# Slot 1's expert weights by a list, issued from Pool's queue; slot 0's second half behind the first gather

## The chip, the cores and the metric

One core of one Trainium2 chip. The metric is the device time of the kernel in microseconds (us). Its five engines are named as in the profile: PE (TensorE, matmuls), DVE (VectorE), ACT (ScalarE), POOL (GpSimd) and SP (SyncE, here only an issuer of DMAs). A "q" behind an engine (ACTq) is its instruction queue.

## The reference, cut to what matters

The whole kernel computes two blocks of two layers each (attention, convolution, gating mixers). The change touches only the mixture-of-experts part, which runs twice (l = 0 and l = 1), each time on 1024 tokens of width 1024 with 32 experts in four groups, two experts of one group for each token:

```python
def moe_ffn(h, w_rg, b_rg, w_re, b_re, w_gate, w_up, w_down):
    ...
    expert = g_idx[:, None] * EXPERTS_PER_GROUP + top_i.astype(jnp.int32)
    ...
    def expert_block(args):
        xblk, e = args
        hid = jax.nn.silu(xblk @ w_gate[e]) * (xblk @ w_up[e])
        return hid @ w_down[e]

    yb = lax.map(expert_block, (xb, block_e)).reshape(n_rows, d)
    return jnp.zeros_like(h).at[row_tok].add(yb * row_w[:, None])
```

w_gate and w_up are 1024x512 for each expert, w_down 512x1024, all float32. Which expert a token takes depends on the data, so the kernel computes its tables on the chip.

## The kernel before

**Tiling.** The 2048 assignments are cut into blocks of 64 rows that share one expert, experts with most blocks first. Counting the assignments of the reference on its inputs gives, for l = 0, 50 blocks (17 experts with one block, 12 with two, 3 with three), and for l = 1, 48 blocks (20, 8 and 4 experts). The blocks are worked off in rounds of two: in round j slot 0 takes block j from the heavy end, slot 1 takes block n + j, where n is the number of rounds (25 and 24). Slot 0 so works through experts of two and three blocks, slot 1 through experts of mostly one.

**Weights.** Each slot has one buffer for one expert: first half of gate and up (a, 2048 KB), second half (b, 2048 KB), down (d, 2048 KB). `load_gu` (L2298) and `load_dn` (L2303) issue them. There is no second buffer: a part can be loaded only when the last matmuls that read it are done. PE counts that in `free_a`, `free_b` and `free_d` (they start at 2 and grow by one for each slot in each round).

**SP** (`blocks_sp`) loads slot 0 from a list: one entry for each new expert, with its expert number (AT_E) and its place (AT_POS). That is 11 loads of a, b, d for l = 0 and 10 for l = 1. With rounds counted from 0, slot 0 takes a new expert in rounds 0, 3, 6, 9, 11, 13, 15, 17, 19, 21, 23 (l = 0) and 0, 3, 6, 9, 12, 14, 16, 18, 20, 22 (l = 1).

**ACT** (`round_act`) loads slot 1 anew in every round, 49 times in all, whether the expert changes or not: a right after slot 1's a matmuls, b right after its b matmuls, d after its down matmuls. It also applies Silu, copies half of the turned rows, and stores the results (`store_y`, four DMAs of 128 KB a round, L2379).

**Pool** (`blocks_pool`) gathers the 128 token rows of a round (512 KB, indirect DMA, L2315, its index copied at L2312) into the one buffer xb, as soon as PE has turned the rows before (semaphore `xt`).

**PE** (`blocks_pe`) does in each round: gate and up of slot 0 (a, then b), of slot 1 (a, then b), all at L2345; the turning of `hid` (L2352) and of the next round's rows (`turn_x`, L2329); down of slot 0, down of slot 1 (L2362). Each part waits for its weights with a count that comes from a table (slot 0, AT_RANK) or from the round number (slot 1).

**Tables.** `route_dve` and `route_pe` build them before the rounds from the counts: `fresh` marks a block with a new expert on slot 0, a matmul with `before` ranks them, `one_l` turns them into lists, and PE puts the lists into one row (L2092 to L2094) that DVE copies to `moe_tab`. `in_blk` and `at_off` (L2100) give the token rows of each block, `moe_i` the place at which `sum_pool` later picks each result up.

## Time and profile before

| | us |
|---|---|
| median of 3 runs | 4387.5 |
| lowest, highest | 4382.78, 4392.72 |
| the profiled execution | 4384.98 |
| its span, first to last instruction | 4383.2 |

| engine | busy us | share of the span |
|---|---|---|
| PE | 3946.5 | 90% |
| DVE | 1444.3 | 33% |
| ACT | 898.6 | 21% |
| POOL | 125.6 | 3% |

The rounds of l = 0 run from 2526.2 to 3143.6 of the span, those of l = 1 from 3718.6 to 4310.0. All DMAs together move 693.44 MB. PE's busy share says little by itself: it is an average over stages, and a matmul at half clock counts as busy for twice as long. What the change can do is read from the two stretches of rounds: how long a round takes in which nothing is waited for, and which rounds are longer.

### The profile page before, as it was taken

The numbers are of one execution on the slowest core, as the hardware profiler recorded it, in microseconds if no ns is written. First come the engines' busy times: TensorE is split into PE (matmuls) and PEld (weight loads), VectorE is DVE, ScalarE is ACT, GpSimd is POOL, SyncE is SP. The second block draws the span as 40 slices with busy tenths as digits, with TensorE's granted clock in tenths as the row PEclk, the third lists the DMA queues.
The fourth block names the chain that finished last, engine by engine and source line by source line (L and its number), as shares of the span: only waits on it lengthen the run. The fifth ranks groups of instructions, "written<-read, shape, count | busy, mean of one in ns | idle before, by whom it ended". The sixth has DMA issues, their size and how long they took to land.

```text
span 4383.2 us, 48965 instructions
## 1 busy us (share of the span) xinstructions
PE 3946.5 (90%) x19350; PEld 1970.3 (45%) x19351; DVE 1444.3 (33%) x2688; ACT 898.6 (21%) x1885; POOL 125.6 (3%) x203
## 2 busy tenths in 40 slices
PE   4997888899999889999988799999799997999986
PEld 2555665454444555444664333333344443333333
DVE  2485666313302663252463411111231114111115
ACT  3003454202001332121152211111120002111111
POOL 0000000000000000000000000000100000000001
PEclk8998999999999999999999899999899998999997
DMA  6310222110101000110240299999711103999995
GB/s 244 136 39 36 94 94 112 44 42 33 62 20 39 1 1 10 48 46 30 97 156 20 84 399 378 426 426 424 312 36 39 39 21 130 385 391 392 420 423 200
DMA packets 81279, 693.44 MB, mean 158 GB/s; under 512 B 9696, under 2 KB 11560, under 8 KB 45408
## 3 DMA queue, kind: packets, MB, share of 16 engines
q10 hardware_dynamic: 39824, 342.78, 19.0%
q1 hardware_dynamic: 23168, 280.66, 16.0%
q0 software_dynamic: 18128, 67.77, 4.2%
q8 instruction: 114, 1.87, 0.2%
q14 instruction: 45, 0.37, 0.0%
HBM read 636.11 MB, written 55.05 MB: 158 GB/s over the span
## 4 chain that ended last, share of the span: by engine, by line
PE 44%; DMA 11%; DVE 4%; issue 1%; ACT 1%; POOL 0%; ACTq 0%; DVEq 0%; POOLq 0%
PE banks L259 22%; PE banks L2345 12%; DMA arena<-in_w_gu 10%; PE banks L2362 5%; PE banks L1476 1%; DMA arena<-y_tok,arena 1%; DVE arena L1591 1%; PE banks L2329 1%; PE banks L2067 1%; PE banks L2352 1%; DMA arena<-h_tok,arena 1%; PE banks L466 1%; PE banks L1545 0%; PE banks L1525 0%; DVE banks L1590 0%
## 5 line engine op out<-in xcount | busy, mean ns | idle before, releaser
L259 PE MATMUL banks<-arena 128*128 128x512 f32 (+2 forms) x4544 | 1752.2, 547 | 50.4 <-ACTq L138 28.7
L259 PEld LDWEIGHTS banks<-arena 128*128 128x128 f32 x4544 | 841.6, 191 | 950.4 <-issue 887.5
L2345 PE MATMUL banks<-arena 128*64 128x512 f32 x3136 | 718.4, 615 | 70.8 <-DMA arena<-in_w_gu 68.5
L2345 PEld LDWEIGHTS banks<-arena 128*64 128x64 f32 x3136 | 231.4, 142 | 548.2 <-issue 456.8
L2362 PE MATMUL banks<-arena 128*64 128x512 f32 x1568 | 349.2, 598 | 3.2 <-issue 3.2
L1545 PE MATMUL banks<-arena 128*64 128x128 f32 x1952 | 162.1, 285 | 54.5 <-ACT arena L1558 39.3
L2362 PEld LDWEIGHTS banks<-arena 128*64 128x64 f32 x1568 | 109.0, 137 | 208.5 <-issue 208.5
L939 DVE SCALAR_TENSOR_TENSOR arena<-arena 128x1024 f32<-128x1024 f32 x240 | 195.9, 878 | 0.2 <-DVEq L138 0.2
L2435 DVE COPY arena<-banks 128x256 f32<-128x256 f32 x98 | 41.1, 420 | 414.4 <-PE banks L2352 414.4
L1476 PE MATMUL banks<-arena 64*128 64x256 f32 (+2 forms) x768 | 130.1, 469 | 37.8 <-ACT arena L1647 32.8
L301 DVE SCALAR_TENSOR_TENSOR arena<-banks,arena 128x512 f32<-128x512 f32 (+1 forms) x72 | 51.9, 721 | 333.7 <-PE banks L259 333.7
L1525 PE MATMUL banks<-arena 128*128 128x128 f32 x976 | 150.5, 285 | 1.9 <-ACT arena L1647 1.9
L1545 PEld LDWEIGHTS banks<-arena 128*64 128x64 f32 x1952 | 103.2, 136 | 106.0 <-ACT arena L1558 78.3
L2431 DVE TENSOR_TENSOR arena<-arena,banks 128x256 f32<-128x256 f32 x98 | 40.8, 416 | 325.4 <-ACT arena L2385 325.4
L272 ACT ACTIVATE arena<-banks 128x512 f32<-128x512 f32 (+1 forms) x43 | 24.1, 559 | 577.5 <-PE banks L259 577.5
L2439 DVE COPY arena<-banks 128x512 f32<-128x512 f32 x49 | 33.9, 692 | 324.1 <-PE banks L2362 324.1
L1273 PE MATMUL banks<-arena 128*128 128x128 f32 x800 | 109.4, 285 | 34.5 <-DVE arena L1364 34.5
L1647 ACT ACTIVATE arena<-banks,arena 128x1024 f32<-128x1024 f32 (+3 forms) x144 | 135.2, 939 | 23.0 <-DVE arena L1593 22.1
L1591 DVE TENSOR_REDUCE arena<-banks 128x1 f32<-128x1024 f32 (+3 forms) x144 | 135.4, 940 | 13.2 <-PE banks L1476 9.5
L1525 PEld LDWEIGHTS banks<-arena 128*128 128x128 f32 x976 | 104.8, 142 | 55.4 <-issue 50.1
L280 ACT ACTIVATE arena<-banks 128x512 f32<-128x512 f32 (+1 forms) x68 | 38.0, 559 | 424.6 <-PE banks L259 424.5
L1558 ACT ACTIVATE arena<-banks 128x512 f32<-128x512 f32 (+1 forms) x160 | 90.6, 566 | 163.5 <-PE banks L1525 162.2
(341 smaller groups left out, 3075.3 us busy)
## 6 DMA issues: line engine op xcount, KB each, us to landing
arena<-in_w_gu ACTq DMA_DIRECT2D x98, 2048.0 KB, 14.0
arena<-in_w_dn ACTq DMA_DIRECT2D x49, 2048.0 KB, 13.2
arena<-in_w_gu SPq DMA_DIRECT2D x42, 2048.0 KB, 12.3
arena<-in_w_ada SPq DMA_DIRECT2D x24, 2048.0 KB, 7.3
arena<-in_w_dn SPq DMA_DIRECT2D x21, 2048.0 KB, 14.9
y_tok<-arena ACTq DMA_DIRECT2D x196, 128.0 KB, 12.7
y_tok<-arena POOLq DMA_DIRECT2D x1, 16384.0 KB, 45.2
arena<-in_ab_w_ada SPq DMA_DIRECT2D x6, 2048.0 KB, 9.4
```

The costliest lines, as they stand in the source:

```text
L259: last = pe.matmul(self.bank_of(g, n), lhsT, rhs, start=k == 0, stop=k == KT - 1)
L301: d.scalar_tensor_tensor(out=grp.dst, in0=src, scalar=grp.more["gate"], in1=grp.dst, op0=ALU.mult, op1=ALU.add).then_inc(proj_ev["D"], 1)
L939: d.scalar_tensor_tensor(out=out, in0=src, scalar=wt, in1=out, op0=ALU.mult, op1=ALU.add).then_inc(conv_n, 1)
L1273: last = pe.matmul(bank(7)[:, 0:V.shape[1]], self.PT[0:K, g % self.n_pt, 128 * j:128 * j + 128], V, start=g == mine[0] and j == 0, stop=g ...
L1476: ins = pe.matmul(banks[:, c0:c0 + k.shape[1]], q, k, start=True, stop=True)
L1525: ins = pe.transpose(self.tbank(g)[:, 128 * j:128 * j + 128], self.P[u % 2][s_][:, c0:c0 + P], ident)
L1545: ins = pe.matmul(bank(7)[64 * s_:64 * s_ + 64, 0:128], V, self.PT[g % len(self.PT)][:, 128 * j:128 * j + 128], start=g == mine[0] and j < ...
L1558: last = eng.tensor_copy(o, s_) if which == "D" else eng.activation(o, s_, ACT.Copy)
L1591: link(d.tensor_reduce(st[:, s_:s_ + 1], sc[:, 0:un["n"]], X_AXIS, ALU.max))
L1647: a.activation(self.P[i % 2][s_][:, 0:un["n"]], self.scores(s_)[:, 0:un["n"]], ACT.Exp, bias=st[:, 2 + s_:3 + s_], scale=un["scale"][s_][0 ...
L2345: last = pe.matmul(bank(2 + s_)[64 * h:64 * h + 64, :], xbT[:, k, 64 * s_:64 * s_ + 64], w_gu[s_][:, k, h], start=k == 0, stop=k == KT - 1 ...
L2362: last = pe.matmul(bank(6 + s_)[64 * h:64 * h + 64, :], hidT[:, s_, ch % 2, 64 * (ch // 2):64 * (ch // 2) + 64], w_dn[s_][:, ch, 512 * h:5 ...
```

## The change

- The blocks of slot 1 run backwards: in round r it takes block 2n - 1 - r instead of n + r, so from the light end. Equal experts of slot 1 so still stand side by side, but the experts with two blocks come last.
- `fresh`, the ranks and the lists are made for both slots. Slot 1's list has, besides the expert and the first round of each entry, the round behind its last one (AT_END). Slot 1 is loaded only for a new expert.
- ACT loads no weights any more, and its round has one form. Pool issues slot 1's weights: after the gathers of the rounds that an entry covers, a and b when `free_a` and `free_b` allow it, then d when `free_d` does.
- The gather of round j + 2 stands in iteration j, behind `xt` j + 2; one more gather is issued at the end of each stage (27 and 26 instead of 26 and 25).
- On SP, part b of slot 0 waits for the first gather (`xg` 16); in later iterations that wait is always met.
- PE waits for slot 1's weights by a rank from the table, as for slot 0.
- The tables need some more small steps on DVE (`n_last`, `before_of`, a second `one_l`, `held`, the ranks, and five for the new place of each result) and slightly other matmuls.

```diff
@@ route_pe
+                both_l = one_l.rearrange("p a b -> p (a b)")
+                for at_, col in ((AT_E, exp_id), (AT_POS, place[:, 0:1])):
+                    pe.matmul(bank(7)[0:1, at_:at_ + 2 * LOADS], col, both_l, start=True, stop=True)
+                pe.matmul(bank(7)[0:1, AT_END:AT_END + LOADS], place[:, 0:1], one_l[:, 1], start=True, stop=False)
+                pe.matmul(bank(7)[0:1, AT_END:AT_END + LOADS], place[:, 1:2], held, start=False, stop=True)
...
@@ route_dve
-                link(d.tensor_scalar(blk_of, side, rounds_n[0:NBLK], first_round, ALU.mult, ALU.add))
+                link(d.tensor_scalar(n_last, rounds_n, 2.0, -1.0, ALU.mult, ALU.add))
+                link(d.tensor_scalar(blk_of, side, n_last[0:NBLK], from_end, ALU.mult, ALU.add))
+                link(d.scalar_tensor_tensor(out=before_of, in0=side, scalar=2.0, in1=blk_of, op0=ALU.mult, op1=ALU.add))
...
-                link(d.tensor_scalar(one_l, c("iota", NBLK)[:, 0:LOADS], rank, fresh, ALU.is_equal, ALU.mult))
-                d.tensor_tensor(rank, rank, fresh, ALU.add).then_inc(m_oh, 1)
+                for s_ in range(2):
+                    link(d.tensor_scalar(one_l[:, s_], c("iota", NBLK)[:, 0:LOADS], rank2[:, s_:s_ + 1],
+                                         fresh2[:, s_:s_ + 1], ALU.is_equal, ALU.mult))
+                link(d.tensor_tensor(rank2, rank2, fresh2, ALU.add))
+                link(d.tensor_scalar(held, c("iota", NBLK)[:, 1:LOADS + 1], rank2[:, 1:2], valid, ALU.is_equal,
+                                     ALU.mult))
+                link(d.tensor_tensor(rank, rank2[:, 1:2], rank2[:, 0:1], ALU.subtract))
+                d.tensor_scalar(rank, rank, side, rank2[:, 0:1], ALU.mult, ALU.add).then_inc(m_oh, 1)
...
+                link(d.tensor_scalar(places[:, 1], iota_r, -1.0, n_last, ALU.mult, ALU.add))
...
@@ blocks_sp
                     for part, landed, free in ((0, self.wa[0], self.free_a), (1, self.wb[0], self.free_b)):
+                        if part == 1:
+                            sp.wait_ge(self.xg, 16)
                         sp.wait_ge(landed, 16 * j + 16)
                         sp.sem_inc(self.passed, 1)
-                        sp.wait_ge(free, pos + 1)
+                        sp.wait_ge(free, 2 * pos + 1)
...
@@ blocks_pool
-                with g.Fori(0, n) as j:
-                    g.wait_ge(self.xt, j + 1)
-                    self.gather(g, j + 1)
+                more = g.value_load(moe_tab[0:1, AT_ROUNDS + 1:AT_ROUNDS + 2], min_val=1, max_val=LOADS - 1)
+                e = g.value_load(moe_tab[0:1, AT_E + LOADS:AT_E + LOADS + 1], min_val=0, max_val=E - 1)
+                g.wait_ge(self.xt, 1)
+                self.gather(g, 1)
+                for part in range(2):
+                    self.load_gu(g, 1, e, part)
+                self.load_dn(g, 1, e)
+                with g.Fori(0, more) as i:
+                    first = g.value_load(moe_tab[0:1, bass.ds(AT_POS + LOADS + i, 1)], min_val=0, max_val=ROUNDS - 1)
+                    end = g.value_load(moe_tab[0:1, bass.ds(AT_END + i, 1)], min_val=1, max_val=ROUNDS)
+                    e = g.value_load(moe_tab[0:1, bass.ds(AT_E + LOADS + 1 + i, 1)], min_val=0, max_val=E - 1)
+                    with g.Fori(first, end) as j:
+                        g.wait_ge(self.xt, j + 2)
+                        self.gather(g, j + 2)
+                    for part, free in ((0, self.free_a), (1, self.free_b)):
+                        g.wait_ge(free, 2 * end + 2)
+                        g.sem_inc(self.passed, 1)
+                        self.load_gu(g, 1, e, part)
+                    g.wait_ge(self.free_d, 2 * end + 2)
+                    g.sem_inc(self.passed, 1)
+                    self.load_dn(g, 1, e)
...
@@ blocks_pe
-                    rank_ = pe.value_load(moe_tab[0:1, bass.ds(AT_RANK + 2 * j, 1)], min_val=1, max_val=LOADS)
-                    need = [16 * rank_ + 16, 16 * j + 16]
+                    ranks = [pe.value_load(moe_tab[0:1, bass.ds(AT_RANK + 2 * j + s_, 1)], min_val=1, max_val=LOADS)
+                             for s_ in range(2)]
+                    need = [16 * ranks[0] + 16, 16 * ranks[1]]
...
@@ round_act, blocks_act
-                if not last:
-                    a.wait_ge(self.free_a, 2 * j + 4)
-                    self.load_gu(a, 1, e, 0)
...
-                if not last:
-                    self.load_gu(a, 1, e, 1)
...
-                if not last:
-                    a.wait_ge(self.free_d, 2 * j + 4)
-                    self.load_dn(a, 1, e)
...
```

## Rows read from the trace of the kernel before

**Rows 1.** The page, part 4: the chain that ended last, by line.

```profile
PE banks L259 22%; PE banks L2345 12%; DMA arena<-in_w_gu 10%; PE banks L2362 5%; PE banks L1476 1%; DMA arena<-y_tok,arena 1%; DVE arena L1591 1%; PE banks L2329 1%; PE banks L2067 1%; PE banks L2352 1%; DMA arena<-h_tok,arena 1%; PE banks L466 1%; PE banks L1545 0%; PE banks L1525 0%; DVE banks L1590 0%
```

**Rows 2.** Waits of the whole kernel: who for whom: us in total, times, longest.

```profile
PE banks L2345 <- DMA arena<-in_w_gu: 68.5, 24, 4.3
```

**Rows 3.** Windows: rounds of each layer, rounds after the first, single stretches.

```profile
core 0: us, PE busy (x) PEld busy (x) DVE busy (x) ACT busy (x) POOL busy (x), PEclk, DMA share, GB/s
2526.20:3143.60 617.40, 579.40 (x2700) 205.79 (x2700) 71.49 (x149) 79.81 (x124) 28.48 (x49) 0.97 0.97 405
3718.60:4310.00 591.40, 557.66 (x2592) 197.07 (x2592) 68.61 (x143) 76.46 (x119) 27.43 (x47) 0.97 0.95 393
2550.20:2988.50 438.30, 414.64 (x1946) 146.97 (x1944) 51.97 (x108) 58.38 (x90) 20.73 (x36) 0.98 0.98 408
3743.70:4258.80 515.10, 485.60 (x2272) 172.13 (x2270) 60.64 (x126) 68.12 (x105) 24.13 (x42) 0.97 0.97 401
2839.00:2889.80 50.80, 46.96 (x220) 16.39 (x218) 5.78 (x12) 6.49 (x10) 2.31 (x4) 0.97 1.01 426
2608.68:2615.30 6.62, 6.62 (x17) 1.80 (x18) 0.00 (x0) 0.00 (x0) 0.00 (x0) 0.55 1.03 434
```

**Rows 4.** Timeline of a quiet round: start, length (us), engine, line, operation.

```profile
2550.20 13.90 PE L2345 MATMUL banks<-arena 128*64 128x512 f32 x64
2550.55 0.34 ACTq L2303 DMA_DIRECT2D arena<-in_w_dn  x1
2560.85 0.35 ACTq L2298 DMA_DIRECT2D arena<-in_w_gu  x1
2564.30 0.34 ACTq L2298 DMA_DIRECT2D arena<-in_w_gu  x1
2564.31 1.04 PE L2329 MATMUL banks<-arena 128*128 128x128 f32 x8
2565.68 7.09 PE L2362 MATMUL banks<-arena 128*64 128x512 f32 x32
2566.49 0.97 POOL L2315 DMA_INDIRECT arena<-h_tok,arena  x1 [0.79 <-POOL arena L2312]
2572.60 1.46 PE L2345 MATMUL banks<-arena 128*64 128x512 f32 x6
```

**Rows 5.** Timeline of the next round: SP's loads of slot 0.

```profile
2576.45 3.77 SPq L2298 DMA_DIRECT2D arena<-in_w_gu  x2
2591.99 0.33 SPq L2303 DMA_DIRECT2D arena<-in_w_dn  x1
```

**Rows 6.** Timeline of the round after that: the stall.

```profile
2608.68 6.62 PE L2345 MATMUL banks<-arena 128*64 128x512 f32 x16 [3.21 <-DMA arena<-in_w_gu]
```

**Rows 7.** DMA issues at 2634.4 and 2507.4 alone: last column, us to landing.

```profile
arena<-in_w_gu ACTq DMA_DIRECT2D x1, 2048.0 KB, 7.2
...
arena<-in_w_gu SPq DMA_DIRECT2D x1, 2048.0 KB, 8.1
```

**Rows 8.** DMA queues from 2576 to 2606: packets, MB, share.

```profile
q1 hardware_dynamic: 431, 6.29, 49.4%
q0 software_dynamic: 144, 0.52, 4.3%
```

**Rows 9.** The page, part 6: issues of gate and up halves, median us to landing.

```profile
arena<-in_w_gu ACTq DMA_DIRECT2D x98, 2048.0 KB, 14.0
arena<-in_w_gu SPq DMA_DIRECT2D x42, 2048.0 KB, 12.3
```

**Rows 10.** Timeline ahead of the first round of layer 1.

```profile
2499.77 0.14 DVE L2240 COPY arena<-banks 64x1 f32<-64x1 f32 x1
2505.92 3.63 PE L2100 MATMUL banks<-arena 128*64 128x33 f32 x64 [3.01 <-DVE arena L2258]
2511.01 1.05 POOL L2315 DMA_INDIRECT arena<-h_tok,arena  x1 [0.87 <-POOL arena L2312]
2522.89 1.97 PE L2329 MATMUL banks<-arena 128*128 128x128 f32 x8 [13.35 <-DMA arena<-h_tok,arena]
```

More of the change, by code:

```diff
@@ L2217, in route_dve @@
                 link(d.tensor_copy(ends, bank(7)[:, 0:65]))
-                first_round, side = (c("place", NBLK)[:, i:i + 1] for i in range(2))
+                first_round, side, from_end = (c("place", NBLK)[:, i:i + 1] for i in range(3))
                 upto = ends[0:NBLK, 32:64]
@@ L2320, in blocks_pool @@
                 n = self.rounds(g)
-                with g.Fori(0, n) as j:
-                    g.wait_ge(self.xt, j + 1)
-                    self.gather(g, j + 1)
+                more = g.value_load(moe_tab[0:1, AT_ROUNDS + 1:AT_ROUNDS + 2], min_val=1, max_val=LOADS - 1)
[19 more added lines that the diff above has]
+                    self.load_dn(g, 1, e)
+                first = g.value_load(moe_tab[0:1, bass.ds(AT_POS + LOADS + more, 1)], min_val=0, max_val=ROUNDS - 1)
+                with g.Fori(first, n) as j:
+                    g.wait_ge(self.xt, j + 2)
+                    self.gather(g, j + 2)
+                g.wait_ge(self.xg, 16 * n + 32)
+                g.sem_inc(self.passed, 1)
             def turn_x(self, pe, j):
```

100 lines of the change are left out of this document (46 added, 54 removed).

## The prediction

> **What bounds the kernel now.** I read the chain that ended last first: outside the dense projections (L259) it runs through the expert matmuls L2345 (12%) and L2362 (5%) and through the DMA of `in_w_gu` (10%) [rows 1]. So both PE and the weight loads end stretches of the rounds. The waits then say how much PE really idled for them: 68.5 us in 24 waits, none over 4.3 us [rows 2]. The windows give the size of the whole matter. The rounds take 617.4 and 591.4 us [rows 3]. A quiet round is 22.40 us, from 2550.20 to 2572.60 [rows 4], and 49 of them are 1097.6 us. So 1208.8 - 1097.6 = 111.2 us are lost in the rounds, and no change of the loads alone can win more than these.
>
> Where they are lost: in the windows without the first round, 18 rounds of l = 0 take 438.3 us, 35.1 over the quiet time, with 7 reloads of slot 0; 21 rounds of l = 1 take 515.1, 44.7 over, with 8 reloads [rows 3]. That is 79.8 us, **5.3 us for each of 15 reloads**. The other 31.4 us lie in the two first rounds and around the last four reloads. A stall looks so: the second half of slot 1 comes 3.21 us late [rows 6], and behind it 6.62 us run at a granted clock of 0.55, near the lower of the two levels (1.2 and 2.4 GHz) [rows 3]; before, PE had been idle for those 3.21 us. 68.5 us of waits and some 43 us of slow matmuls make the 111.
>
> Two rounds with one reload take 50.8 us at 426 GB/s and a DMA share of 1.01 [rows 3]: there the transfers themselves are the bound. Over the first 18 rounds after the opening the rate is 408: where the reloads are three rounds apart, there is room, and stalls come from order, not from amount.
>
> **The clock of a round.** From the quiet round [rows 4], counted from its start: PE's four quarters of L2345 end at 3.5, 6.9, 10.4 and 13.9 (13.90 in four equal parts); the turning of rows ends at 15.2 (2565.35); down begins at 15.5, its second half at 19.0. Slot 1's loads are issued at 10.7 (a), 14.1 (b) and 0.4 of the next round (d). The gather is issued from 16.3 to 17.3. SP issues a at 3.9 and, within that row of 3.77 us, b at about 7.3, and d at 19.4 [rows 5]. Weights are due: slot 1's a at 6.9, b at 10.4, d at 19.0; slot 0's a at 0. A load alone lands 7.2 to 8.1 us after its issue [rows 7]; 2048 KB at 426 GB/s are 4.9, so 2.3 to 3.2 are fixed. I take 1.6 ahead of the first byte and 1.3 behind the last, near the upper end, because the row of SP is the load that nothing shared with. When two queues hold loads, each gets about half (the medians are 14.0 and 12.3 us against 7.2 alone [rows 9]).
>
> **Part 1: slot 1's a and b leave later.** Today ACT issues them right after the quarter that frees the buffer. In the new order Pool must first wait for the turning of the rows and issue the gather, which ends at 17.3. The two loads follow: Pool's price for issuing a plain 2048 KB load is not in these rows; its bounds are ACT's 0.34 and the gather's 0.97 us [rows 4]. I take 0.9, nearest to the row of the same engine. So a leaves at 18.2 instead of 10.7 and b at 19.0 instead of 14.1: **7.5 and 5 us later**, in a round in which both are due 11 and 14 us after that. They also stand on one queue behind the gather, and d of this round behind them.
> - A round with nothing from SP: gather 18.9 to 20.1, a to 25.0, b with the y stores (0.52 MB, 1.2 us) to 31.2, landing 26.3 and 32.5; due 29.3 and 32.8. No stall, but only 0.3 us to spare for b.
> - The round ahead of a reload (SP issues at 3.9 and 7.3): b has 2.7 us left to move when SP's a enters at 5.5. At half rate, with stores, it lands near 13; due 10.4, stall 2.7. d follows at half rate, 11.8 to 21.7, lands at 23.0; due 19.0 + 2.7, stall 1.3 to 1.7. Neither is long enough for a lower clock, if the stall of 3.21 us is the measure. Together **4.4**, and this round has no loss today.
> - The reload round: SP's b and d are still moving while the gather and slot 1's a want to. The gather has small packets (0.52 MB in 144, against 6.29 MB in 431 on SP's queue [rows 8]) and, packet by packet in turn, is pushed to about 28; a moves at half rate beside SP's d and lands at 37.8 from the start of the round before, due at 26.8 + 6.9 = 33.7. Stall 4.1, then slow matmuls: 43 us over 19 reloads are 2 us each. Together **6.0**.
>
> So 10.4 us for a reload instead of 5.3, and over 15 reloads 156 - 79.8 = **+76 us**. The same by amount: behind the reload round all loads are done some 5 us before Pool issues the next gather, and in a stretch where the DMAs are the bound those 5 us are lost.
>
> **Part 2: fewer loads.** Backwards, slot 1's 25 rounds of l = 0 hold 17 single experts and four of two rounds: 21 loads. For l = 1 it is 20 and two: 22. 43 instead of 49, each 6.29 MB, 14.8 us at 426 GB/s. But the six that go lie in rounds 18, 20, 22, 24 and 21, 23, behind the stretch where the DMAs are the bound. In the last four reloads (19, 21, 23 and 22) both slots want weights in the same round: a of slot 1, leaving at 18.2 beside SP's d, lands 1.8 late, b 3.1 late, with 2 for the clock 6.8, so 27 us for four. Today they and the two first rounds lose 31.4. I take **0**; the ends are -27 (all gone) and +14.
>
> **Part 3: the start.** Today the gather is issued at 2511.0 beside three loads of slot 0 and PE starts at 2522.9, 13.35 us idle [rows 10]. With only a ahead of it the rows land near 2516.5, 6 us sooner. But b of slot 0 leaves then, and slot 1's a waits for the turning and for gather 1, whose small packets stand beside SP's b and d: it moves from about 2527 and lands near 2535.5, where today the second quarter ends at 2534. The 6 us become a stall of about 7 plus slow matmuls. **+3.5 for each l, +7**; ends -4 and +10.
>
> **Part 4: the tables.** Ahead of the release of the rounds stand 6 more chained steps on DVE: the row at 2499.77 is 0.14 long and the next is chained at 0.18 [rows 10], some 0.22 with its wait. 1.3 us for each l, **+2.6**. The five steps for the place of the results lie beside PE's 3.63 us at 2505.92 [rows 10]; without that cover they would cost 1.1 each time. ACT's loop gets lighter, but ACT is not waited for. The extra gather at the end lies beside the last round. SP's new wait holds only SP's own b and d, priced in part 3.
>
> **Sum.** 76 + 0 + 7 + 2.6 = +86 on the profiled execution's 4385.0: 4471. The median of the runs shown is 2.5 above it: **4473 us**, own range 4440 to 4505 (the fixed part of a load 2.3 instead of 2.9, or Pool's issue 0.5 us slower, moves it by some 10 each; the ends of parts 2 and 3 by some 25).
>
> **Rivals.**
> - *The later issue is hidden by what is queued.* At a DMA share of 1.01 it should not matter when a load joins the queue. Then only the six loads and the last four reloads count: -27 and +2.6, 4363. For: the two-round stretch. Against: SP's two halves are all that is queued at 18, and rounds with nothing from SP are quiet until 17. The Trainium skill ("DMA: Bandwidth & Descriptors", section "Issuing engines are not separate DMA queues") says that the issuing engine saves only issue time, since all share 16 DMA engines; by it the move to Pool is neutral. Chance 0.13. That even the other 84 us go, 4280: 0.02.
> - *Half of it.* Backlog covers the lateness where reloads are two rounds apart, and only the seven reloads three rounds apart lose 5: +35 with parts 3 and 4 and less of part 2, 4420. Chance 0.08, with 4388, no difference, inside its lower edge.
> - *Slower still: Pool's packets are smaller than SP's.* Pool's gathers average 3.6 KB, SP's loads 14.6 [rows 8]. If Pool's weight loads are cut to half of SP's packets, slot 1 gets a third beside SP instead of half. b is then 6.4 late in the round ahead of a reload (8.3 with the clock), and a 3.2 late after it (5.1): 13.4 instead of 10.4, +45, 4518. It decides once the packets differ by two. No plain load of such rows by Pool is in these rows. Chance 0.13.
> - *Forecast* 0.64.
>
> **How the numbers follow.** The likeliest is 4473. Leaving out the 0.15 on the fast side and the tails gives 4410 to 4530. A measurement of this kernel can tell 0.2% (8.8 us) from no change: faster 0.15, same 0.02, slower 0.83.
>
> **What the profile after would show.** Queue q0 with some 339 MB, q10 with 34 (342.78 less 49 times 6.29), 37.7 MB less in all; Pool's loads at about 18 and 19 of a round; new waits of L2345 and L2362 in the round ahead of each reload, near 27 us, and reload rounds near 28.5; rounds 18, 20, 22 at 22.4. Wrong, if the round ahead of a reload stays at 22.4 (then the backlog covers it), or if Pool's a leaves before 15.

## The result, and the profile after

| | before | changed kernel |
|---|---|---|
| median us | 4385.14 (4 runs, 4374.65 to 4392.72) | 4459.68 (4 runs, 4458.66 to 4460.59) |
| the profiled execution | 4384.98 | 4459.17 |
| its span | 4383.2 | 4457.3 |

The ratio is 1.0172, 95% interval 1.015 to 1.0194: the changed kernel is 74.5 us slower. The forecast was 86 slower, 4473. The time is 13 below it and inside the range.

From the page of the changed kernel: PE's busy time, and two of the DMA queues (packets, MB, share). L2388 is now the gate and up matmul, L2405 down, L2371 the turning of rows, L2333 the gather, L2319 and L2324 the weight loads.

```profile
PE 3965.0 (89%) x19354; PEld 1981.0 (44%) x19355; DVE 1448.0 (32%) x2710; ACT 900.9 (20%) x1886; POOL 200.6 (5%) x337
...
q0 software_dynamic: 36992, 339.36, 19.0%
...
q10 hardware_dynamic: 18656, 34.49, 2.2%
```

Queue q0 carries 339.36 MB and q10 34.49, as the prediction had them. All DMAs together move 656.74 MB instead of 693.44, so 36.7 MB less. The prediction said 37.7, because it left out the two extra gathers of 0.52 MB. **Less is moved and it takes longer**: PE is only 18.5 us busier over the whole span, the rest of the loss is idle time. PE's waits for gate and up weights went from 68.5 us [rows 2] to

```profile
PE banks L2388 <- DMA arena<-in_w_gu: 106.9, 24, 8.7
```

in as many waits, the longest twice as long. Where they lie, the windows say (stretch, us, then each engine's busy time, granted clock, DMA share, GB/s): the rounds of l = 0 and of l = 1, their rounds after the first up to the last stretch (two lines), the last stretches (two lines), and in the end a quiet round, the round ahead of a reload and the reload round.

```profile
2520.10:3177.00 656.90, 592.58 (x2700) 212.15 (x2700) 71.47 (x149) 80.69 (x125) 64.70 (x114) 0.94 0.85 349
3748.10:4380.50 632.40, 567.54 (x2592) 202.82 (x2592) 68.66 (x143) 77.51 (x120) 65.06 (x115) 0.95 0.86 355
2553.10:3021.50 468.40, 423.24 (x1946) 152.32 (x1944) 51.96 (x108) 58.39 (x90) 48.82 (x87) 0.95 0.90 372
3782.50:4328.80 546.30, 494.32 (x2270) 177.67 (x2268) 60.61 (x126) 68.12 (x105) 57.23 (x102) 0.96 0.90 370
3021.50:3177.00 155.50, 142.24 (x650) 50.73 (x646) 17.32 (x36) 19.46 (x30) 10.94 (x19) 0.93 0.70 278
4328.80:4380.50 51.70, 47.65 (x218) 16.48 (x214) 5.76 (x12) 6.49 (x10) 2.88 (x5) 0.93 0.49 187
2553.10:2575.50 22.40, 22.40 (x110) 8.11 (x108) 2.89 (x6) 3.24 (x5) 2.80 (x5) 1.00 0.82 332
2575.50:2599.50 24.00, 22.55 (x110) 8.21 (x108) 2.88 (x6) 3.24 (x5) 2.80 (x5) 1.00 1.00 424
2599.50:2628.80 29.30, 24.32 (x110) 8.69 (x108) 2.89 (x6) 3.24 (x5) 2.80 (x5) 0.94 0.89 363
```

Against [rows 3]: 468.4 instead of 438.3 us and 546.3 instead of 515.1, so +61.3 us for the same 15 reloads. DMA share and rate fell from 0.98 and 408 GB/s to 0.90 and 372. The last stretches are 0.4 and 0.5 longer than before (155.1 and 51.2). In all rounds, span less PE busy is 129.2 us of idle time, before 71.7: +57.5. PE's busy time is 1160.1 against 1137.1: +23.0, the same matmuls at a lower clock.

The timeline of these three rounds (start, length, engine, line, operation, idle time ahead and who ended it):

```profile
2570.40 1.09 POOL L2319 DMA_DIRECT2D arena<-in_w_gu  x2
2591.79 0.99 POOL L2333 DMA_INDIRECT arena<-h_tok,arena  x1 [0.79 <-POOL arena L2330]
2592.79 1.09 POOL L2319 DMA_DIRECT2D arena<-in_w_gu  x2
2594.89 0.33 SPq L2324 DMA_DIRECT2D arena<-in_w_dn  x1
2596.09 3.65 PE L2405 MATMUL banks<-arena 128*64 128x512 f32 x16 [1.45 <-issue]
2599.54 7.07 PE L2388 MATMUL banks<-arena 128*64 128x512 f32 x32
2611.48 8.82 PE L2388 MATMUL banks<-arena 128*64 128x512 f32 x32 [4.87 <-DMA arena<-in_w_gu]
```

Pool issues a and b right behind the gather (2570.40), 17.3 and 17.8 us after the round's start. In the next round the same group leaves at 2592.79, when SP's b (issued at 2582.8) still moves and SP's d is about to join (2594.89). a should be there for the third quarter at 2606.6. It is there at 2611.48, 4.87 us late; the 32 matmuls behind it take 8.82 us instead of 7. In the round ahead, the second half of down starts 1.45 us late. The view names no releaser, but slot 1's d lands at 2596.00, right ahead of it. And because PE is late, the next gather is issued only at 2622.69, when everything queued has been moved: the channels nearly stand still from 2621.6 to 2624.6 (19 GB/s).

```profile
2621.60:2624.60 3.00, 3.00 (x16) 1.12 (x18) 1.01 (x2) 0.58 (x1) 2.08 (x4) 1.00 0.21 19
```

How long the gather takes (last column: us to landing; the quiet round's gather and the reload's):

```profile
arena<-h_tok,arena POOLq DMA_INDIRECT x1, 4.4
...
arena<-h_tok,arena POOLq DMA_INDIRECT x1, 11.3
```

The 512 KB of rows land in 4.4 us alone and in 11.3 beside SP's loads, as the prediction had expected from its small packets (said to be pushed to 28 of the round before, measured 27.6).

### The profile page after: what moved, and what is told of

Read it like the earlier page. It is cut to its first block, busy times and chain, and to the rows that moved or that the text cites. A ratio compares the mean times of both kernels' runs of the same rounds, so it can differ in the third digit from the quotient of the medians.

```text
span 4457.3 us, 49754 instructions
## 1 busy us (share of the span) xinstructions
PE 3965.0 (89%) x19354; PEld 1981.0 (44%) x19355; DVE 1448.0 (32%) x2710; ACT 900.9 (20%) x1886; POOL 200.6 (5%) x337
## 2 busy tenths in 40 slices
DMA packets 78976, 656.74 MB, mean 147 GB/s; under 512 B 9441, under 2 KB 11305, under 8 KB 45409
## 3 DMA queue, kind: packets, MB, share of 16 engines
q0 software_dynamic: 36992, 339.36, 19.0%
q1 hardware_dynamic: 23168, 280.66, 15.8%
q10 hardware_dynamic: 18656, 34.49, 2.2%
## 4 chain that ended last, share of the span: by engine, by line
PE 44%; DMA 11%; DVE 4%; issue 2%; ACT 1%; POOLq 1%; POOL 0%; DVEq 0%; ACTq 0%
PE banks L259 22%; PE banks L2388 12%; DMA arena<-in_w_gu 10%; PE banks L2405 4%; PE banks L2371 1%; PE banks L1476 1%; DMA arena<-y_tok,arena 1%; DVE arena L1591 1%; PE banks L2395 1%; PE banks L2071 1%; PE banks L466 1%; DMA arena<-h_tok,arena 0%; PE banks L1545 0%; PE banks L1525 0%; POOLq L138 0%
## 5 line engine op out<-in xcount | busy, mean ns | idle before, releaser
L2388 PE MATMUL banks<-arena 128*64 128x512 f32 x3136 | 740.3, 630 | 109.0 <-DMA arena<-in_w_gu 106.9
L2388 PEld LDWEIGHTS banks<-arena 128*64 128x64 f32 x3136 | 242.4, 146 | 597.4 <-issue 453.8
L2405 PE MATMUL banks<-arena 128*64 128x512 f32 x1568 | 350.8, 596 | 22.1 <-issue 22.0
L2405 PEld LDWEIGHTS banks<-arena 128*64 128x64 f32 x1568 | 110.1, 137 | 227.8 <-issue 227.8
L2434 ACT ACTIVATE arena<-banks 128x256 f32<-128x256 f32 x98 | 37.6, 383 | 639.7 <-PE banks L2388 639.7
L1476 PE MATMUL banks<-arena 64*128 64x256 f32 (+2 forms) x768 | 130.2, 470 | 37.7 <-ACT arena L1647 32.8
L1545 PEld LDWEIGHTS banks<-arena 128*64 128x64 f32 x1952 | 103.0, 136 | 106.7 <-ACT arena L1558 78.4
L272 ACT ACTIVATE arena<-banks 128x512 f32<-128x512 f32 (+1 forms) x43 | 24.1, 559 | 579.0 <-PE banks L259 579.0
L1558 ACT ACTIVATE arena<-banks 128x512 f32<-128x512 f32 (+1 forms) x160 | 90.6, 566 | 164.4 <-PE banks L1525 162.3
## 6 DMA issues: line engine op xcount, KB each, us to landing
arena<-in_w_gu POOLq DMA_DIRECT2D x86, 2048.0 KB, 14.8
y_tok<-arena ACTq DMA_DIRECT2D x196, 128.0 KB, 10.4
```

Of the source, the lines that this page charges most:

```text
L1476: ins = pe.matmul(banks[:, c0:c0 + k.shape[1]], q, k, start=True, stop=True)
L1545: ins = pe.matmul(bank(7)[64 * s_:64 * s_ + 64, 0:128], V, self.PT[g % len(self.PT)][:, 128 * j:128 * j + 128], start=g == mine[0] and j < ...
L1558: last = eng.tensor_copy(o, s_) if which == "D" else eng.activation(o, s_, ACT.Copy)
L2388: last = pe.matmul(bank(2 + s_)[64 * h:64 * h + 64, :], xbT[:, k, 64 * s_:64 * s_ + 64], w_gu[s_][:, k, h], start=k == 0, stop=k == KT - 1 ...
L2405: last = pe.matmul(bank(6 + s_)[64 * h:64 * h + 64, :], hidT[:, s_, ch % 2, 64 * (ch // 2):64 * (ch // 2) + 64], w_dn[s_][:, ch, 512 * h:5 ...
```

## The experiments

All times are medians, with the ratio to the runs of before on the same chip. "Reload" is a reload round less 22.4 us, mean over the 15 reloads of the two long windows; "ahead" is the same for the round before it (before: 5.3 and 0.0; changed kernel: 7.6 and 1.8); "last four" is the sum over the last four reloads (before 26.8, changed kernel 27.5).

### Lateness alone, on ACT's queue

The kernel before, with slot 1's a and b issued behind ACT's copy of the turned rows.

```diff
-                if not last:
-                    a.wait_ge(self.free_a, 2 * j + 4)
-                    self.load_gu(a, 1, e, 0)
                 a.wait_ge(self.free_b, 2 * j + 4)
                 ...
-                if not last:
-                    self.load_gu(a, 1, e, 1)
                 self.copy_x(a, "A", j + 1)
+                if not last:
+                    a.wait_ge(self.free_a, 2 * j + 4)
+                    for part in range(2):
+                        self.load_gu(a, 1, e, part)
```

> The kernel before with one move: ACT issues slot 1's a and b (still in every round, still on its own queue) behind its copy of the turned rows instead of right behind each quarter. They leave at about 16 of a round instead of 10.7 and 14.1. Theory of lateness: the round ahead of a reload and the reload round together lose 8 to 9 us over 44.8 instead of 5.3; over 19 reloads 35 to 65 us slower than before. Rival, Pool's queue (software descriptors, one queue for gather, a, b and d) is the cause of the loss: nothing is moved to Pool here, so within 9 us of before. Rival, the backward order and the list are the cause: within 9 us of before too.

4415.08 us, ratio 1.0067 (1.005 to 1.0084): 31.5 slower. Reload 7.1, ahead 0.0, last four 32.8. In the round ahead of the first reload, a and b leave 15.3 and 15.8 us after its start; in the changed kernel it is 17.3 and 17.8, so this run tests most of the lateness and not all of it. The windows: the rounds of both layers.

```profile
2525.90:3163.70 637.80, 587.00 (x2700) 206.24 (x2700) 71.46 (x149) 79.83 (x124) 28.45 (x49) 0.96 0.95 392
3736.00:4341.10 605.10, 562.11 (x2592) 198.02 (x2592) 68.59 (x143) 76.44 (x119) 27.42 (x47) 0.96 0.93 384
```

Idle time of the rounds is 93.8 us, 22.1 more than before, and PE is busy 12.0 longer. So a load that joins the queue later is not hidden by what stands in it: the backlog rival is wrong. But this much lateness on ACT's queue gives less than half of the loss, and it never reaches the round ahead of a reload.

### Pool's queue alone, and Pool late

Weights for every round as before (no list), a and b on Pool when their part comes free, gather and d behind them. ACT issues no weights any more, and slot 1's first three loads leave behind the second gather:

```diff
@@ blocks_pool
+                with g.Fori(0, before) as j:
+                    e = self.expert(g, j + 1)
+                    for part, free in ((0, self.free_a), (1, self.free_b)):
+                        g.wait_ge(free, 2 * j + 4)
+                        g.sem_inc(self.passed, 1)
+                        self.load_gu(g, 1, e, part)
+                    g.wait_ge(self.xt, j + 2)
+                    self.gather(g, j + 2)
+                    g.wait_ge(self.free_d, 2 * j + 4)
+                    g.sem_inc(self.passed, 1)
+                    self.load_dn(g, 1, e)
```

> The kernel before, slot 1 still loaded in every round and in forward order, but all its loads issued by Pool, a and b as early as ACT did (behind their quarters, ahead of the gather), d behind the gather; the first three leave behind gather 1. Theory of lateness: the rounds lose about what they lose before, 95 to 125 us over the quiet time in all, so 4375 to 4400. Rival, Pool's queue is the cause: 60 us or more above before, near 4445 to 4460, with a stall of a in each reload round.

4366.93 us, ratio 0.9956 (0.9941 to 0.997): 16.6 **faster** than before. Reload 3.7, ahead 0.0, last four 25.8. The second kernel only moves the turning's wait and the gather ahead of a and b, where the change has them:

```diff
                     e = self.expert(g, j + 1)
+                    g.wait_ge(self.xt, j + 2)
+                    self.gather(g, j + 2)
                     for part, free in ((0, self.free_a), (1, self.free_b)):
                     ...
                         self.load_gu(g, 1, e, part)
-                    g.wait_ge(self.xt, j + 2)
-                    self.gather(g, j + 2)
```

> As the run above, but the gather ahead of a and b, as in the changed kernel; still 49 loads in forward order, no list. Theory of lateness: rounds 1 to 18 (l = 0) and 1 to 21 (l = 1) lose what they lose in the changed kernel, some 9.4 us for each of 15 reloads, and the last four reloads 9.4 each as well: 4460 to 4480, 0 to 15 above the changed kernel. Rival, the list with its backward order is the cause: near before, 4375 to 4400.

4474.79 us, ratio 1.0203 (1.0186 to 1.022). Reload 7.4, ahead 2.0, last four 47.5 (their rounds ahead included). The windows of the rounds of both layers: Pool early with its first reload round, then that reload round of before, then Pool late.

```profile
2527.80:3143.70 615.90, 575.51 (x2700) 203.21 (x2700) 71.45 (x149) 80.74 (x125) 69.59 (x124) 0.98 0.97 407
3719.00:4291.90 572.90, 543.82 (x2592) 192.91 (x2592) 68.58 (x143) 77.56 (x120) 66.83 (x119) 1.00 0.97 406
2599.80:2625.80 26.00, 22.61 (x110) 7.95 (x108) 2.88 (x7) 3.25 (x5) 2.79 (x5) 1.00 1.01 430
```
```profile
2595.00:2623.90 28.90, 25.69 (x112) 8.77 (x110) 2.89 (x6) 3.24 (x5) 1.15 (x2) 0.88 1.01 426
```
```profile
2531.40:3200.60 669.20, 596.62 (x2700) 212.48 (x2700) 71.46 (x149) 80.77 (x125) 70.02 (x124) 0.95 0.90 374
3776.50:4404.10 627.60, 566.70 (x2592) 202.68 (x2592) 68.57 (x143) 77.51 (x120) 67.25 (x119) 0.95 0.89 371
```

**The order on Pool costs 108 us** (4366.9 to 4474.8) with every load still made and on one queue. That is the change's loss, and more than it. Pool early against before shows something else. Idle time in the rounds is 69.5 us against 71.7, nearly the same, and so is the rate in the reload round (430 and 426 GB/s). What is shorter is PE's busy time, 1119.3 against 1137.1. In the first reload round the stall is 3.4 us (26.00 less 22.61 busy) and the clock stays at 1.00, where before a stall of 3.2 was followed by matmuls at 0.55 [rows 3, 6].

One pair of rounds doesn't tell the whole. Over the 15 reload rounds of the two long windows, the granted clock lies below 1.00 in 11 before and in 3 with Pool early (in the changed kernel in all 15). And the waits have another form. Before, the wait for slot 1's second half takes 2.5 to 3.9 us (in 3 rounds with a shorter one for its first half ahead of it). With Pool early PE waits twice in 8 of the 15, for slot 0's second half and for slot 1's, mostly under 2 us each, and in 5 of the other 7 the one wait takes 1.8 to 2.2 us. A round of l = 1:

```profile
4100.50 7.09 PE L2359 MATMUL banks<-arena 128*64 128x512 f32 x32 [1.84 <-DMA arena<-in_w_gu]
4109.48 3.65 PE L2359 MATMUL banks<-arena 128*64 128x512 f32 x16 [1.90 <-DMA arena<-in_w_gu]
```

So the waits of a reload are cut into shorter pieces (3.0 us in all on average, before 3.5), and the clock falls less often. That the shorter pieces are the cause is not shown: in the kernel before, one wait of 3.9 us (round 16 of l = 1) left the clock at 1.00, and in the kernel with all of slot 1 on Pool's queue, shown further down, one of 2.0 us (round 9 of l = 1) was followed by 0.94 over the round.

### The gather behind the late weights

As the kernel before it (Pool late), but only the wait for the turning stays ahead; the gather follows a and b.

```diff
                     g.wait_ge(self.xt, j + 2)
-                    self.gather(g, j + 2)
                     for part, free in ((0, self.free_a), (1, self.free_b)):
                     ...
                         self.load_gu(g, 1, e, part)
+                    self.gather(g, j + 2)
```

> As the run with Pool late and no list (4474.8): a and b still wait for the turned rows, but the gather is issued behind them instead of ahead. Splits what lateness on ACT's queue left open (31 us there, 91 with Pool late). If the gather's small packets ahead of a on one queue are the other part: a reload costs 6 to 7.5 us instead of 9.4, total 4415 to 4445. Rival, Pool's queue with d behind a and b is that part (or the late issue alone, to be read as 9.4 on any queue): above 4460.

4453.1 us, ratio 1.0162 (1.0134 to 1.019). Both expectations fell: the time lies between. Reload 7.1, ahead 1.3. Of the loss in the rounds against Pool early (90.9 us over quiet rounds there, 176.9 here, 198.9 with the gather ahead), 86 come from leaving late and 22 from the gather ahead of the weights on the same queue. Leaving late cost only 34 on ACT's queue (from 111 over quiet rounds before to 145). One difference lies in the round ahead of a reload: there the second half of down starts 1.3 us late on average in this kernel and in time in the one on ACT's queue. Here d stands behind a, b and the gather on one queue, there the gather has a queue to itself. No run separates that from the 0.7 us by which a and b also leave later here (16.0 instead of 15.3).

### The wait at the start

The changed kernel without SP's wait for the first rows.

```diff
-                        if part == 1:
-                            sp.wait_ge(self.xg, 16)
```

> The changed kernel without SP's wait of slot 0's second half for the first gather. Only the start of the rounds can differ. By the working of the start: the first gather again shares with three loads, PE starts some 6 us later (near 2526), slot 1's first a leaves later too, the stall in front of it is shorter: total 0 to 6 us above the changed kernel. Rival, the wait costs what the first round has lost (33 us against 24): 5 to 15 us below the changed kernel.

4460.32 us, ratio 1.0176 (1.0159 to 1.0193). From SP's first issue to round 1 it takes 44.3 and 45.9 us, with the wait 45.3 and 46.1, before 42.8 and 43.1. The wait moves TensorE's start 6 us earlier and gives it all back in the first round:

```profile
2507.83 9.85 SPq L2319 DMA_DIRECT2D arena<-in_w_gu  x2
2517.07 1.97 PE L2371 MATMUL banks<-arena 128*128 128x128 f32 x8 [7.00 <-DMA arena<-h_tok,arena]
2521.09 1.15 POOL L2319 DMA_DIRECT2D arena<-in_w_gu  x2
```

This is the changed kernel's start. SP's line of 9.85 us is its a and, behind the wait, its b. The rows are there after 7.00 us of idling instead of 13.35 [rows 10], but slot 1's first weights leave at 2521.09, behind the turning and the second gather.

### The last gather

The changed kernel without the extra gather at the end of each stage.

```diff
-                with g.Fori(first, n) as j:
+                with g.Fori(first, n - 1) as j:
                     g.wait_ge(self.xt, j + 2)
                     self.gather(g, j + 2)
-                g.wait_ge(self.xg, 16 * n + 32)
+                g.wait_ge(self.xg, 16 * n + 16)
```

> The changed kernel without the one gather that it adds at the end of each stage (its rows are used by nothing). Pool's drain of 7.6 us behind that gather ended 2 us after ACT's. If it holds the stage back: 2 to 3 us less for each l, 4453 to 4456. Rival, ACT's stores set the stage's end anyway: within 1 us of the changed kernel.

4454.25 us, ratio 1.0162 (1.0134 to 1.019), 5.4 below the changed kernel's median. The timeline at the end of l = 1: in the changed kernel the last matmuls and the first gather of the results, and then that gather in this kernel and in the kernel before.

```profile
4377.77 2.75 PE L2405 MATMUL banks<-arena 128*64 128x512 f32 x12
4387.34 0.95 POOL L2470 DMA_INDIRECT arena<-y_tok,arena  x1 [12.12 <-POOLq L138]
```
```profile
4383.95 0.97 POOL L2470 DMA_INDIRECT arena<-y_tok,arena  x1 [31.95 <-ACTq L138]
```
```profile
4314.29 0.94 POOL L2447 DMA_INDIRECT arena<-y_tok,arena  x1 [32.00 <-ACTq L138]
```

In the changed kernel Pool waits for **its own queue** (POOLq L138, the meeting of all engines at the stage's end), in the others for ACT's. From the end of the matmuls it is 6.8 us to the gather instead of 4.3 and 4.3; for l = 0 it is 6.6 instead of 4.4 and 4.3. Pool's part of that meeting (its drain, in the records of its sequencer) takes 7.57 us, begun 1.5 us ahead of the last matmul's end. It takes as long without the extra gather (7.49), but begins 24.2 us ahead of that end; before, it took 10.72 and began 28.8 us ahead. So it cost nothing there.

### The list with early weights

The changed kernel with slot 1's a and b issued for the next entry as soon as `free_a` and `free_b` allow, ahead of the gathers, and d on ACT's queue.

```diff
@@ blocks_pool, for entry i + 1 of the list
                     for part, free in ((0, self.free_a), (1, self.free_b)):
-                        g.wait_ge(free, 2 * end + 2)
+                        g.wait_ge(free, 2 * first + 2)
                         g.sem_inc(self.passed, 1)
                         self.load_gu(g, 1, e, part)
-                    g.wait_ge(self.free_d, 2 * end + 2)
-                    g.sem_inc(self.passed, 1)
-                    self.load_dn(g, 1, e)
+                    with g.Fori(first, end) as j:
+                        g.wait_ge(self.xt, j + 1)
+                        self.gather(g, j + 1)
@@ blocks_act, behind the rounds of entry i
+                    a.wait_ge(self.free_d, 2 * end + 2)
+                    a.sem_inc(self.passed, 1)
+                    self.load_dn(a, 1, e)
```

> The changed kernel (list, backward order, 43 loads) with slot 1's a and b issued by Pool ahead of the gather, as early as their buffers are free, and d issued by ACT behind a round. One gather less at the end. Theory of lateness: reload rounds lose 3 to 5 us and the rounds ahead of them nothing, as with Pool early and no list (55 us over 15 reloads), and the last four reloads, which cost 26 us there, lose 0 to 8 in all: 4335 to 4360. Rival, the list or the backward order slows the rounds by itself: above 4385.

4404.82 us, ratio 1.0049 (1.0031 to 1.0067): the expectation missed by 45 us or more. The last four cost 10.4 instead of 26.8, as expected, but the reload still costs 6.6, and the two first rounds 16.5 and 17.6 over a quiet one. A second kernel issued slot 1's first a and b ahead of the second gather and held SP's first d behind them:

```diff
+                    sp.wait_ge(self.wb[1], 16)
                     self.load_dn(sp, 0, e)
@@ blocks_pool
-                g.wait_ge(self.xt, 1)
-                self.gather(g, 1)
                 for part in range(2):
                     self.load_gu(g, 1, e, part)
+                g.wait_ge(self.xt, 1)
+                self.gather(g, 1)
```

> As the run above, with another start: slot 1's first a and b stand right behind gather 0 on Pool's queue, gather 1 behind them, and SP's down loads wait until slot 1's first b has landed (met at once later on). By the working of the start the first round no longer waits 6 to 9 us for slot 1's a behind gather 1 and SP's d: 5 to 12 us below the run above. Rival, the start is bound by the amount to be moved: within 4 us of it.

4404.69 us, ratio 1.0052 (1.0037 to 1.0068): no difference in the time. From SP's first issue to round 1 it takes 50.6 and 49.5 us, in the kernel without these edits 50.7 and 52.3. Both are slow starts: before, the same loads took 42.8 and 43.1. In both, ACT issues slot 1's first d, which is needed last, right behind the first gather (2518.85 in the first kernel). SP's b, issued at 2518.99 and needed early, then lands after 13.2 us. The timeline of a reload in the first of the two kernels shows the rest:

```profile
2605.41 10.79 PE L2380 MATMUL banks<-arena 128*64 128x512 f32 x48
2608.20 0.35 ACTq L2324 DMA_DIRECT2D arena<-in_w_dn  x1
2618.69 5.35 PE L2380 MATMUL banks<-arena 128*64 128x512 f32 x16 [2.49 <-DMA arena<-in_w_gu]
2630.44 3.65 PE L2397 MATMUL banks<-arena 128*64 128x512 f32 x16 [1.16 <-issue]
```

ACT issues d 2.8 us into the reload round (2608.20, from 2605.41), behind result stores; before it was 0.4 [rows 4]. b comes 2.49 late, and the second half of down stands 1.16 us for d (the view names no releaser). I took this for a theory: d on a third queue takes shares from a and b.

### All of slot 1 on one queue, early

The list and backward order of the change, with a, b, gather and d of slot 1 all on Pool's queue, each when its part comes free, and no extra gather. The loop over entries is split at 17 and 20, the numbers of experts with one block, constants for these inputs.

```diff
@@ blocks_pool
+                single = (17, 20)[self.l]
+                with g.Fori(0, single - 1) as i:
+                    self.next_expert(g, i, i + 1)
...
+            def next_expert(self, g, i, first):
+                e = g.value_load(moe_tab[0:1, bass.ds(AT_E + LOADS + 1 + i, 1)], min_val=0, max_val=E - 1)
+                for part, free in ((0, self.free_a), (1, self.free_b)):
+                    g.wait_ge(free, 2 * first + 2)
+                    g.sem_inc(self.passed, 1)
+                    self.load_gu(g, 1, e, part)
+                g.wait_ge(self.xt, first + 1)
+                self.gather(g, first + 1)
+                g.wait_ge(self.free_d, 2 * first + 2)
+                g.sem_inc(self.passed, 1)
+                self.load_dn(g, 1, e)
```

> The list and the backward order of slot 1 of the changed kernel, with the first rows waited for by SP as there, but all of slot 1's loads on Pool's queue in the order first half, second half, gather, down weights, each issued as its part of the buffer comes free. (The loop over loads is split at the number of experts with one round, 17 and 20 for these inputs, a constant here.) It is the kernel with the early weights alone on Pool's queue (4366.9 us) plus the list. Theory that a third weight queue took the shares in the two kernels with the list and down weights on ACT's queue: reload rounds cost 3.7 us over a quiet one again (they were 6.6), the last four reloads of slot 0, which stand without one of slot 1, cost 8 to 16 us instead of 25.8, the tables cost 3 more; 4345 to 4370. Rival, that the list or the backward order of slot 1 slows the rounds by itself, whatever the queue: reloads stay near 6.6 us and the time is 4385 or more.

**4351.05 us**, ratio 0.9941 (0.9928 to 0.9955): faster than both kernels, 26.5 us below the runs of before beside it. Reload 3.6, ahead 0.0, last four 6.5. The list and the backward order so cost nothing in themselves; against Pool early without a list they are worth 19.3 us in the last four. The two first rounds cost 11.3 and 11.8 us over a quiet one, where they cost 16.5 and 17.6 with d on ACT's queue. The granted clock lies below 1.00 in 5 of the 15 reload rounds, with d on ACT's queue in all 15. First the windows of the rounds of the kernel with d on ACT, then those of this one:

```profile
2521.70:3154.40 632.70, 586.17 (x2700) 211.96 (x2700) 71.53 (x149) 78.60 (x123) 52.12 (x91) 0.96 0.89 362
3725.70:4335.30 609.60, 562.96 (x2592) 203.19 (x2592) 68.72 (x143) 75.35 (x118) 51.99 (x91) 0.96 0.90 367
```
```profile
2516.90:3120.90 604.00, 573.20 (x2700) 204.24 (x2700) 71.49 (x149) 80.80 (x125) 63.45 (x112) 0.98 0.92 379
3691.50:4268.60 577.10, 548.72 (x2592) 194.28 (x2592) 68.70 (x143) 77.56 (x120) 63.88 (x113) 0.98 0.93 388
```

Idle 93.2 us there and 59.2 here, PE busy 1149.1 and 1121.9. In this kernel's first reload, b is 1.81 late and the clock stays up:

```profile
2595.39 10.47 PE L2392 MATMUL banks<-arena 128*64 128x512 f32 x48
2596.31 0.55 POOL L2324 DMA_DIRECT2D arena<-in_w_dn  x1 [6.02 <-PE banks L2409]
2607.67 3.65 PE L2392 MATMUL banks<-arena 128*64 128x512 f32 x16 [1.81 <-DMA arena<-in_w_gu]
```

The queues over the 10.5 us ahead of b's landing, with d on ACT (first) and on Pool (second):

```profile
q0 software_dynamic: 200, 2.23, 49.9%
q1 hardware_dynamic: 128, 1.80, 40.1%
q10 hardware_dynamic: 206, 0.34, 8.5%
```
```profile
q0 software_dynamic: 217, 2.37, 53.3%
...
q10 hardware_dynamic: 219, 0.36, 9.1%
```

My theory was wrong in its detail. d takes no share from b here: b is as late in both, 13.4 and 13.3 us into the reload round on average. But ACT's queue q10 moves only 0.34 MB in these 10.5 us, in 206 packets, while q0 moves 2.23 MB in 200. These are result stores in small packets, and **d, issued at 2608.20, stands behind them**: its large packets begin after 2618. It lands 22.1 us after its issue. Down's second half starts 1.8 us late on average over the 15 reloads with d on ACT, and in time with d on Pool. That the queues hand over about the same number of packets is what the Trainium skill says ("DMA: Bandwidth & Descriptors", section "Queues, rings and completion order": each DMA engine takes its queues in turn, a packet at a time); the trace agrees, 200 and 206. SP's q1 has 128: until 2617 each of the three moves 10 to 16 packets a microsecond, then SP's loads run out while the gather's small packets come. d also leaves earlier on Pool, 0.9 us into the round (2596.31, from 2595.39). How the 1.8 us divide between the later issue and the stores ahead, no run separates.

### The start of that kernel

Two more, from the kernel just shown: without SP's wait for the first rows (the edit shown above), and, with the wait kept, slot 1's first a and b ahead of the second gather:

```diff
-                g.wait_ge(self.xt, 1)
-                self.gather(g, 1)
                 for part in range(2):
                     self.load_gu(g, 1, e, part)
+                g.wait_ge(self.xt, 1)
+                self.gather(g, 1)
                 self.load_dn(g, 1, e)
```

> The kernel with the list and all of slot 1's loads early on Pool's queue (4351.1 us), with SP's wait for the first rows taken out: the second half of slot 0's first weights is issued at once behind the first. There, 45.4 us pass from SP's first issue to round 1 and the first round costs 11.3 and 11.8 us over a quiet one. Theory that both stage starts are bound by the amount to be loaded until round 1: the first rows and the first half of slot 1 land later, TensorE starts later, and round 1 starts within 2 us of where it did; 4346 to 4353. Rival, that the wait leaves the channels idle between the first half and the rows: round 1 starts 4 us earlier or more in each stage, 4343 or less. The other way: the gather is slowed by the 2 MB load beside it so that round 1 is over 2 us later, 4355 or more.

4355.59 us, ratio 0.9942 (0.9931 to 0.9954). Round 1 comes 44.4 and 46.0 us after SP's first issue, with the wait 45.4 and 46.2.

> The same kernel (4351.1 us) with the wait kept, and slot 1's two first weight halves issued on Pool ahead of the second gather, which stood ahead of them. The first half of slot 1 was waited for by 7.1 us in the first round. Theory of the amount: the halves land up to 2 us earlier each, and what stands behind them comes as much later; 4347 to 4353. Rival, that the gather of small rows ahead of them on the queue holds them back (it landed after 10.9 us there): the first rounds lose 3 us or more each and the time is 4345 or less.

4351.52 us, ratio 0.9935 (0.9922 to 0.9947); 44.4 and 45.3 us. Neither order of the start can be told from the other by the time. In these three kernels round 1 comes within 1.0 us of the others, though the waits and the order differ: as if only the amount counted that must land. That isn't so for every order. With slot 1's first d on ACT's queue, early, the same loads took 50.7 and 52.3 us until round 1, here 45.4 and 46.2: there a load that is needed last shared the channels with one that is needed first.

## Why the prediction was right, point by point

**Part 1, the later issue of a and b: right in kind, too large by 15 us.** Forecast 10.4 us for a reload against 5.3, +76; measured 9.4, +61.3. The round ahead was to cost 4.4 and costs 1.8, the reload round 6.0 and costs 7.6. Over 15 reloads that is 39 too many and 24 too few, so the sum is better than its two halves, which is luck.

The term that failed is b's stall of 2.7 us in the round ahead; d's (1.3 to 1.7 said) came as 1.3 to 1.6. The prediction let SP's a enter the channels at 5.5 of that round, 1.6 after its issue at 3.9, when b still had 2.7 us to move. The queues from SP's issue at 2579.35 to 2582.80, in the first of these rounds:

```profile
q0 software_dynamic: 80, 1.31, 88.6%
q10 hardware_dynamic: 80, 0.13, 10.0%
```

SP's queue q1 is not among them. Its first packet comes at 2582.83, 7.3 us into the round, and in all 15 rounds 3.4 to 3.7 us after the issue. The gather's first packet came earlier than said, at 18.0 instead of 18.9 of the round before. So b had 0.26 MB of its 2.10 left when SP's a entered. It landed at 10.0, due 10.4, where the prediction said 13. In 13 of the 15 rounds PE waited no more than 0.2 us for it, in two 0.5 and 0.9 us.

*Pool's price for issuing a load* was mis-sized too: the two loads at 2570.40 take 1.09 us together, 0.55 each, where 0.9 was taken. By the prediction's own clock that moves nothing: the gather's bytes end at 20.1 and a's follow, and both loads are issued before that at either price. The fixed part of a load was the term that mattered, and not as one number: at the start of the stage SP's a moved its first packet 1.0 us after its issue.

The reload round was sized near, and lost more because the round ahead lost less. a lands 35.9 to 36.5 us after the start of the round ahead, where 37.8 was said, but it is due at some 31.1 instead of 33.7. The stall is 4.9 us on average (4.3 to 5.2) against 4.1. In the round shown PE is busy 1.9 us more than in a quiet round (24.32 against 22.40), against 2; the dearest of the 15 costs 8.1 in all. The idle channels that the prediction had by amount are there, but 3 us long in this round (at 19 GB/s) where it said some 5.

**Part 2, fewer loads: right.** 0 was taken between -27 and +14; the last stretches are 0.9 longer, the last four reloads 27.5 us for a forecast of 27. The forecast had a 1.8 and b 3.1 late in each; in fact a was in time in all four and b 3.4 to 6.1 late. The total is a sum of two things: the late kernel without the list loses 47.5 there. The list saves 20 us and the late issue spends them. Issued early, the 20 are had.

**Part 3, the start: near.** Forecast +3.5 for each l, measured +2.5 and +3.0, with PE some 6 us earlier at its first matmul, as said. Slot 1's a landed at 2535.8, forecast 2535.5.

**Part 4, the tables: right, with a gap.** Forecast 1.3 each, measured 1.4 and 1.5 (from DVE's first step of the tables to SP's first issue, 18.88 and 18.20 us instead of 17.46 and 16.74). But "the extra gather at the end lies beside the last round" is the step that failed: the gather itself is hidden, what Pool does behind it at the stage's end is not. It costs 2.3 and 2.5 us, 4.8 in all; without the gather the median is 5.4 lower.

61.3 + 0.9 + 5.5 + 2.9 + 4.8 = 75.4, against 74.2 between the profiled executions. The forecast of +86 came close by an excess of 15 in part 1 and 5 us that it had not seen, which lie on opposite sides.

**The rivals.** *Hidden by backlog* (0.13) fell with the first experiment: no load was dropped or moved to another queue, and lateness cost 31.5 us. Its rule in the Trainium skill ("DMA: Bandwidth & Descriptors", section "Issuing engines are not separate DMA queues": transfers from all engines share the 16 DMA engines, another issuer saves only issue time) is met by the idle time and the rates of Pool early against before (69.5 and 71.7 us, 430 and 426 GB/s), though not by the time: it is 16.6 us less, and PE's busy time 17.8 us less, at a higher granted clock. *Pool's packets smaller* (0.13): they are as large as SP's. The queues over 14.4 us of the kernel with all of slot 1 on Pool, in which Pool issues a and b:

```profile
q1 hardware_dynamic: 257, 3.69, 59.8%
q0 software_dynamic: 161, 2.38, 38.5%
```

2.38 MB in 161 packets are 14.8 KB each, SP's 3.69 MB in 257 are 14.4. The condition was not met. *Half of it* would have needed the close reloads to stay as they were; they lost as the others (rounds ahead 24 to 25 us, reloads 30).

## What to carry to other kernels

When a buffer has no second copy, the place at which its reload is issued is worth more than the amount that is reloaded: here six dropped loads were worth 20 us, and a wait put ahead of the issue cost 86 on Pool's queue and 34 on ACT's. Before moving an issue to another engine, write down what that engine's program makes it wait for, and put each load directly behind the semaphore that frees its buffer, with the gather of the next rows behind it. And look at what an engine has just issued when a stage ends: a last DMA that nobody needs can delay the meeting of all engines.

## What the runs showed that was not expected

- Pool takes 0.55 us for issuing a plain 2048 KB load (two in 1.09), ACT 0.34 [rows 4], though its gather takes 0.99.
- Pool's end of a stage (its drain) takes 7.57 and 10.72 us and is felt when nothing else is later.
- Stalls of nearly the same length (3.2 and 3.4 us, at the same place of a round) were followed by a granted clock of 0.55 in the kernel before and of 1.00 with the weights on Pool's queue. Over all rounds PE's busy time differs by 17.8 us: the clock fell in 11 of 15 reload rounds before and in 3 of 15 there, where the waits are mostly shorter. The cause is open.
- In the changed kernel, SP's load of slot 0 moves its first packet 3.4 to 3.7 us after its issue in the 15 rounds ahead of a reload, and 1.0 us after it at the start of the stage. Why is open.
- The same loads cost 34 us of idle time more or less (93.2 and 59.2), with the down weights of one slot behind the result stores on ACT's queue or behind the gather on Pool's.
